# Expert stages of a two-layer hybrid backbone: the rests of the split weight blocks get places of their own

## What is computed

```python
def expert_block(args):
    hb, eb, gb = args
    a = jnp.einsum('tkd,td->tk', u_tab[eb], hb)
    w = (jax.nn.gelu(a.astype(jnp.float32)) * gb).astype(hb.dtype)
    return jnp.einsum('tk,tkd->td', w, v_tab[eb])
...
for l in range(DEPTH):      # DEPTH = 2
    ...
    x = x + mod[5] * peer_ffn(modulate(rms_norm(x, norm2_g[l]), mod[3], mod[4]),
                              peer_wq[l], peer_keys[l], peer_u[l], peer_v[l])
```

## Time and profile before

| | us |
|---|---|
| median of 3 runs | 5834.54 (5817.51 to 5834.57) |
| the profiled execution | 5836.66 |
| its span | 5834.9 |
| expert stage of layer 0, from its first instruction to the first of the next stage | about 2170 to 3290 |
| expert stage of layer 1 | about 4738 to 5795 |

### The profile page before, as it was taken

One profiled execution on the slowest core, in us unless ns is written; L12 is line 12 of the kernel. 1 busy time (PEld: TensorE's weight loads), 2 busy tenths in 40 slices (PEclk: granted clock), 3 DMA queues, 4 the chain that ended last, 5 costly groups with the idle time before them and its releaser, 6 DMA issues. The chain is left out here.

```text
span 5834.9 us, 69400 instructions
## 1 busy us (share of the span) xinstructions
PE 4834.1 (83%) x23606; PEld 3848.4 (66%) x23606; DVE 4288.8 (74%) x7455; ACT 1814.5 (31%) x3273; POOL 975.0 (17%) x708
## 2 busy tenths in 40 slices
PE   7696738889697869999999778878795669999997
PEld 5385726634575658888888547734674558788886
DVE  1647576767635979999999768658636978888887
ACT  0222311221122753333333221221222743333333
POOL 0000005600000003333333125200000012222221
PEclk9798868999898989999999889989997779999999
DMA  6152317821122569999999548502121369999996
GB/s 226 65 166 76 112 43 265 306 70 61 55 86 94 147 200 352 394 390 385 395 397 396 212 169 311 194 30 93 38 87 36 99 205 342 348 340 342 340 343 230
DMA packets 458724, 1231.49 MB, mean 211 GB/s; under 512 B 210275, under 2 KB 244484, under 8 KB 397382
## 3 DMA queue, kind: packets, MB, share of 16 engines
q1 hardware_dynamic: 357192, 625.56, 30.8%
q0 software_dynamic: 101376, 604.02, 27.3%
HBM read 1169.37 MB, written 60.03 MB: 211 GB/s over the span
## 5 line engine op out<-in xcount | busy, mean ns | idle before, releaser
L2398 POOL DMA_INDIRECT arena<-in_peer_uv,kept x448 | 636.6, 1421 | 3470.6 <-POOLq L2249 1967.2
L233 PE MATMUL psum<-v_ring_hi,w_parts 128*128 128x512 f32 x2560 | 844.4, 394 | 11.5 <-DVE ring_lo L2500 10.9
L233 PE MATMUL psum<-h_hi,u_ring_hi 128*128 128x384 f32 (+1 forms) x2048 | 682.3, 333 | 90.9 <-DVE ring_lo L2495 90.8
L233 PE MATMUL psum<-h_hi,ring_lo 128*128 128x384 f32 (+1 forms) x2048 | 676.3, 330 | 0.0
L233 PE MATMUL psum<-h_lo,u_ring_hi 128*128 128x384 f32 (+1 forms) x2048 | 675.3, 330 | 0.0
L2535 DVE SCALAR_TENSOR_TENSOR arena<-arena 128x1024 f32<-128x1024 f32 x448 | 558.5, 1282 | 19.2
L2525 DVE CUSTOM_DVE_ANT_0 arena<-arena 128x1024 f32<-128x1024 f32 x448 | 536.5, 1220 | 36.9 <-DMA arena<-in_peer_uv,kept 36.4
L233 PEld LDWEIGHTS psum<-v_ring_hi,w_parts 128*128 128x128 f32 x2560 | 480.7, 188 | 120.6 <-DVE ring_lo L2500 17.8
L233 PE MATMUL psum<-ring_lo,w_parts 128*128 128x512 f32 x1280 | 503.0, 393 | 0.0
L233 PEld LDWEIGHTS psum<-h_hi,u_ring_hi 128*128 128x128 f32 x2048 | 395.9, 193 | 134.9 <-DVE ring_lo L2495 67.3
L2500 DVE TENSOR_TENSOR ring_lo<-kept,v_ring_hi 128x1024 fp32r<-128x1024 f32 x256 | 313.7, 1225 | 130.2 <-ACT v_ring_hi L2452 116.2
(11 more groups left out here) (386 smaller groups left out, 9707.4 us busy)
## 6 DMA issues: line engine op xcount, KB each, us to landing
kept<-in_mix SPq DMA_DIRECT2D x312, 512.0 KB
kept<-in_peer_u SPq DMA_DIRECT2D x256, 512.0 KB
kept<-in_peer_uv SPq DMA_DIRECT2D x256, 512.0 KB
kept<-in_ada SPq DMA_DIRECT2D x96, 512.0 KB
gate_scratch<-arena SPq DMA_DIRECT2D x11, 4096.0 KB, 20.8
arena<-gate_scratch SPq DMA_DIRECT2D x64, 384.0 KB
arena<-gate_scratch SPq DMA_DIRECT2D x64, 320.0 KB
spec_scratch<-arena SPq DMA_DIRECT2D x4, 2048.0 KB, 8.5
```

The lines of the kernel that those rows point to most:

```text
L233: done = pe.matmul(out, lhs[x], rhs[y], start=first and j == 0, stop=last and j == 2)
L2398: pool.indirect_dma_start(rows[q % NBUF], None, peer_uv, bass.IndirectOffsetOnAxis(ap=at, axis=0))\
```

## The change

The rests get places of their own: `u_lo` (two tensors of 128 x 1024) and `v_lo` (2 x 1024), in memory that this stage left unused. `rest_u` and `rest_v` write there, and the matmuls read from there. A place of `ring` is then free as soon as its rest has been made, so SP waits for `u_split` and `v_split` (VectorE's rests) in place of `a_ready` and `o_done` (TensorE's products). The v load of pass k is now that of block k + 2. What the load's wait guarded so far, the places of hi and lo, is now guarded by a wait of ScalarE: `round_u` waits for `a_ready` and `round_v` for `o_done` of two blocks before. The next stage's first four loads wait for the same as before.

```diff
+        u_lo = [split_tensor(f"u_lo_{k}", at, 1, 1024) for k, at in enumerate((6144, 8192))]
+        v_lo = split_tensor("v_lo", M0 + 25984, 2, 1024)
...
                         if at_most(b, k, NK - 3):
                             load_u(b, k + 3)
-                        if past(b, k, 1) and at_most(b, k, NK - 1):
-                            sp.wait_ge(o_done.sem, o_done.at(b + k))
-                            sp.dma_start(ring[:, 2 + (k + 1) % 2, :], peer_uv[ds((b + (l * NK + k + 1)) * P, P), D:2 * D])\
-                              .then_inc(loaded[2 + (k + 1) % 2].sem, 16)
+                        if at_most(b, k, NK - 2):
+                            sp.wait_ge(v_split.sem, v_split.at(b + (k + 1)))
+                            sp.dma_start(ring[:, 2 + k % 2, :], peer_uv[ds((b + (l * NK + k + 2)) * P, P), D:2 * D])\
+                              .then_inc(loaded[2 + k % 2].sem, 16)
...
                     def load_u(b, k):
-                        sp.wait_ge(a_ready.sem, a_ready.at(b + (k - 1)))
+                        sp.wait_ge(u_split.sem, u_split.at(b + (k - 1)))
...
-                            last = pe_products(pe, ps[:, 6 + k % 2, 0:T], (u_ring_hi[:, k % 2, c], ring_lo[:, k % 2, c]),
+                            last = pe_products(pe, ps[:, 6 + k % 2, 0:T], (u_ring_hi[:, k % 2, c], u_lo[k % 2][:, 0, c]),
...
-                                                   (v_ring_hi[:, k % 2, c], ring_lo[:, 2 + k % 2, c]), False, end)
+                                                   (v_ring_hi[:, k % 2, c], v_lo[:, k % 2, c]), False, end)
...
                     def round_u(b, k):
                         act.wait_ge(loaded[k % 2].sem, loaded[k % 2].at(8 * b + (16 * (k // 2) + 16)))
+                        if past(b, k, 2):
+                            act.wait_ge(a_ready.sem, a_ready.at(b + (k - 1)))
...
                     def round_v(b, k):
                         act.wait_ge(loaded[2 + k % 2].sem, loaded[2 + k % 2].at(8 * b + (16 * (k // 2) + 16)))
+                        if past(b, k, 2):
+                            act.wait_ge(o_done.sem, o_done.at(b + (k - 1)))
...
-                        dve.tensor_tensor(ring_lo[:, k % 2, :], ring[:, k % 2, :], u_ring_hi[:, k % 2, :].bitcast(F32), ALU.subtract)\
+                        dve.tensor_tensor(u_lo[k % 2][:, 0, :], ring[:, k % 2, :], u_ring_hi[:, k % 2, :].bitcast(F32), ALU.subtract)\
...
-                        dve.tensor_tensor(ring_lo[:, 2 + k % 2, :], ring[:, 2 + k % 2, :], v_ring_hi[:, k % 2, :].bitcast(F32),
+                        dve.tensor_tensor(v_lo[:, k % 2, :], ring[:, 2 + k % 2, :], v_ring_hi[:, k % 2, :].bitcast(F32),
```

More of the change, by code:

```diff
@@ L2426, in outputs @@
                                 c = slice(half * 512, half * 512 + 512)
-                                pe.matmul(ps[0:P // 2, 4 + half, :], w_parts[:, k % 2, 0:P // 2], ring_lo[:, 2 + k % 2, c],
+                                pe.matmul(ps[0:P // 2, 4 + half, :], w_parts[:, k % 2, 0:P // 2], v_lo[:, k % 2, c],
                                           start=False, stop=False)
```

## The result

The changed kernel takes 5751.77 us (median of 4 runs, 5742.12 to 5758.24) against 5834.56 us before: 0.9861 of the time, 95% interval 0.9842 to 0.9880, so 83 us or 1.4% faster. 5742 us was forecast. The profiled execution has a span of 5748.8 us. The number came out nearly as forecast, in part by luck: the term of layer 1 was 12 us too small and that of layer 0 had the wrong sign, 22 us too high, so that the two errors partly cancel, and the reason given for the largest term was wrong.

A forecast was written before the change was run, and what follows sets the result against it. TensorE nearly bounds layer 0; late loads hold layer 1 above its floor. Gains of 82 (layer 1), 6 (layer 0) and 5 us (stage starts), 93 in all, off the profiled 5836.66 us, adjusted to the median, give 5742 us; range 5697 to 5800.

The forecast's parts named there:

- What bounds the kernel now: Expert stages: layer 0 within 0.17 us a pass of TensorE's floor, layer 1 0.87 us above, waiting for loads.
- Instructions and places: Both expert stages: no compute instruction added or removed, rests writing to another place cost 0 more.
- New waits on ScalarE: Rounding of u and v: waiting for the matmuls of two passes ago holds ScalarE no later than today; 0.
- Layer 1, 82 us: Expert stage of layer 1: earlier v and u loads cut a pass from 8.10 to 7.45 us, 82 us gained.
- so the DMA engines become the bound: Layer 1: a pass costs the DMA engines 7.45 us, above TensorE's 7.23, so they set the pace.
- The signs that the prediction had named for being right: Layer 1: DMA share near 1 at about 368 GB/s, 136.5 us idle down to a third, paired loads.
- Layer 0, 6 us gained: Expert stage of layer 0: only the order of loads and gathers changes; 6 us gained, ends 21 gained or lost.
- will be mostly through by then: Layer 0: the u load, issued earlier, is mostly done when the gather VectorE waits for starts; part of 6 us.
- third rival: Layer 0: loads in front of gathers starve them, 93 us net lost, about 5928 us; chance 0.05.
- Start of the stages, 5 us: Start of both expert stages: the third u block comes earlier, ending ScalarE's idling; 5 us gained, ends 0 and 10.
- TensorE is the bound in layer 1: Rival, layer 1: fuller queues don't slow packets, a pass takes 7.23 us, about 5715 us; chance 0.20.
- The rate hardly rises: Rival, layer 1: a 358 GB/s ceiling gives 7.66 us a pass, 55 us gained, about 5769 us; chance 0.17.

The follow-up runs named there:

- the four kernels that take it apart: Changed kernel with both loads on the old waits (5827.98 us), only u early (5823.97), only v early (5798.99), early loads in layer 1 alone (5739.96).
- the kernel with u in front: Against the kernel with early loads in layer 1 alone: layer 1's u load stands before the v load on the SP queue; 5711.92 us.
- the new order: Against the changed kernel: VectorE makes the rests of u and w before the dot products of the gathered rows; 5740.42 us.

## Why the prediction was right, and where not

*What bounds the kernel now.* Right. Layer 0 stood near TensorE's pace, layer 1 did not, and what kept it was the two loads. The floors read from the SP queue (8.38 and 7.23 us) are within 0.04 us of what kernels without idle time of TensorE reached (8.35 and 8.38 us in layer 0, 7.19 us in layer 1).

*Instructions and places.* 0 was taken; the kernel with new places and old waits shows it (0.9995, 0.9977 to 1.0013).

*New waits on ScalarE.* 0 was taken, and among ScalarE's waits after the change none is of a rounding of u or v on TensorE, in neither stage.

*Layer 1, 82 us.* The term measured 94 us ((8.13 - 7.38) x 126), up to 24 of them by the clock that came back, which the prediction left out. The mechanism, earlier issue, is shown by the four kernels that take it apart. The size rested on the step "so the DMA engines become the bound" at 7.45 us, and this step is wrong: the engines carried what 7.19 us a pass needs, in the kernel with u in front. What really left 0.16 to 0.19 us a pass was named one paragraph earlier in the prediction and then not used: that v's lead exceeds its wait by far, and u's by 0.7 us only. The waits after are the waits for u. That the pass with u late (7.38 us) lies so close to the supposed limit of the DMA engines (7.45 us) is luck. The signs that the prediction had named for being right came true in layer 1 all the same: a share of 0.98 at 372 GB/s, the idle before the two rests down to 45.5 of 136.5 us, loads in pairs. They fit the late u load as well as full DMA engines, so they could not tell the two apart; moving one load could.

*Layer 0, 6 us gained.* It lost 16 us (8.57 to 8.69 us a pass), within the end of 21 us lost, but with the other sign. The step that failed is that the u load "will be mostly through by then": it goes out at 2807.28, 2.1 us before the second gather at 2809.41, and takes 6.8 us to land in the median, so the two still run side by side. The sign that the prediction had named for its third rival, a wait for gathers well over 34 us, came (49.3 us), and the stage was 1.4% longer where it had allowed 1%. The small form of the third rival came true: the gathers wait. Its reason, bytes in front of the gathers, is at most a small part, since a u block half as large or a gate load of a twelfth freed at most 8 of 46 us of waiting. Shown is that the second gather has no slack: with 1.8 us more of it, and the rest of u out of its way, the same landings cost nothing. Why it is late more often after the change is left open. The kernel with v alone early shows that little is enough: counted from the start of the rest of v, its v load goes out after 1.41 us, where with the old waits it is 0.6 to 0.8 us (medians), the gate load follows it as before, and the u load stays where it was.

*Start of the stages, 5 us.* In layer 1 3.9 us (3.7 expected). In layer 0 ScalarE's 1.32 us of idling are gone, but the first pass took 24.1 us against 24.2 us, so they gave nothing in this pair; the other kernels with u's old wait had 24.3 to 25.6 us.

*Sum.* 94 - 16 + 4 = 82 us in the two stages where 82 + 6 + 5 = 93 us were forecast; the spans differ by 86 us. (In the prediction "the ceiling of the third rival" is that of the second, and the 7 us in its widest gain is worked out nowhere; its term for the start ends at 10.) Of the two large rivals, "TensorE is the bound in layer 1" turned out to be the true limit, which one move of a load away from the changed kernel reaches. "The rate hardly rises" (358 GB/s) was refuted: 372 GB/s after, 387 with u in front. HBM Reference of the Trainium skill (Specifications (TRN2)) says that a core streaming alone gets well above its share of about 358 GB/s; the windows shown here of kernels with early loads and all bytes agree (372 to 387 GB/s in layer 1, 384 to 401 in layer 0).

## What to carry to other kernels

A DMA share of 0.98 or 0.99 doesn't say that the DMA engines are the bound: in one stage 0.99 went with 376 GB/s, and 1.00 with 387 when one load had been moved; in the other 0.98 went with 385, and 1.01 with 401 when the use of the gathered rows had been. Ask instead, for each kind of transfer, how long before its use it is issued and how long it takes to land, and compare the smallest lead with the latest landing; in the changed kernel this names the load or gather that is late in both layers. Then ask what stands behind the wait: a late gather cost nothing once the rest that TensorE needs was made before it. When a place is freed earlier, look at what then stands in front of the load on its queue, and which transfer beside it has no slack.

## What was not expected of the hardware

Fewer bytes did not make the engines less busy in proportion: with half of each u block in layer 0, 357 GB/s were moved at a share of 0.97, and with all of it 385 at 0.98 and, in the new order, 401 at 1.01. The mean time of a packet changes with the pattern: in layer 0, 2220 to 3220 us, a load's packet of 4 KB took 163 ns with the old loads, 178 ns with the early ones and 193 ns with half blocks of u, while a gather's packet of 8 KB went from 334 to 316 and 339 ns. The median is the same in all three (159 and 309 ns), so some packets take much longer and most don't. What decides which wasn't tried.
